# Moving the DRAM to DRAM copies of a rolling cache from the projection stage to the MLP stage, in eight rounds

## The reference

```
q, k, v  = project(rmsnorm(x))                       # one matrix, dilated heads a and differential heads b
h        = x + [dilated_attention(a), diff_attention(b)] @ w_out
y        = final_norm(h + relu(rmsnorm(h) @ w_up)**2 @ w_down)      # w_up 1024x4096, w_down 4096x1024
win_k_sample = concat(state_win_k, k_new)[:, 4:]     # (8, 2048, 512) float32; the same for v
```

## Time and profile before

| what | us |
|---|---|
| median of 3 runs (4608.19 to 4615.78) | 4612.5 |
| profiled execution, first to last instruction (span) | 4601.9 |
| projection / prompt attention / decode attention / MLP | about 712 / 1088 / 881 / 1921 |
| PE busy, of the span | 4152.4 (90%) |
| DVE / ACT / POOL busy | 2403.4 / 1536.3 / 805.8 |
| DMA traffic over the span | 686.79 MB, mean 149 GB/s |

### The profile page before, as it was taken

How to read it: one execution, slowest core, us unless ns; L and a number is a source line. 1 busy time by engine, 2 the same in 40 slices (tenths; PEclk the granted TensorE clock), 3 DMA queues, 4 the chain that set the end, 5 groups by cost and what they waited for, 6 DMA issues and landing times. The chain is left out here.

```text
span 4601.9 us, 72420 instructions
## 1 busy us (share of the span) xinstructions
PE 4152.4 (90%) x22272; PEld 3160.3 (69%) x22272; DVE 2403.4 (52%) x5184; ACT 1536.3 (33%) x2569; POOL 805.8 (18%) x694
## 2 busy tenths in 40 slices
PE   7996998999989897888888879999999998999998
PEld 6875884445444444445444458988988997998898
DVE  3333334756677684444444435565565555555654
ACT  2221224555545443223322332233223223223322
POOL 0001000000000000333333322222222222222121
PEclk9997999999999998999999989999999999999999
DMA  5756623110111103999999953324333333332231
GB/s 187 234 194 211 228 76 86 36 37 8 36 35 37 36 10 114 376 330 350 365 348 349 360 171 120 116 95 128 127 100 113 124 110 103 125 118 99 94 125 61
DMA packets 347208, 686.79 MB, mean 149 GB/s; under 512 B 27769, under 2 KB 185465, under 8 KB 343610
## 3 DMA queue, kind: packets, MB, share of 16 engines
q1 hardware_dynamic: 291295, 448.03, 29.3%
q0 software_dynamic: 47488, 218.01, 13.3%
q10 hardware_dynamic: 8155, 17.77, 1.4%
HBM read 632.85 MB, written 117.70 MB: 163 GB/s over the span
## 5 line engine op out<-in xcount | busy, mean ns | idle before, releaser
L1379 POOL TENSOR_TENSOR d_up_lo<-d_up_raw,d_up_hi 128x2048 fp32r<-128x2048 f32 x100 | 460.6, 4606 | 1420.3 <-ACT d_up_hi L1516 1420.3
L1384 PE MATMUL d_ups<-d_a_hi,d_up_hi 128*128 128x416 f32 x1600 | 568.2, 355 | 16.9 <-DVE d_a_lo L1671 16.2
L1386 PE MATMUL d_ups<-d_a_hi,d_up_lo 128*128 128x416 f32 x1600 | 566.1, 354 | 0.0
L836 POOL DMA_DIRECT2D c_v<-in_v_cache x512 | 275.2, 537 | 1638.9 <-issue 1627.8
L1385 PE MATMUL d_ups<-d_a_lo,d_up_hi 128*128 128x416 f32 x1600 | 560.6, 350 | 0.0
L530 PE MATMUL b_s<-b_k,b_q 128*128 128x512 f32 (+3 forms) x1280 | 498.5, 547 | 54.1 <-DVE b_part L662 30.6
L1384 PE MATMUL d_dps<-d_u_hi,d_down_hi 128*128 128x416 f32 x1280 | 461.7, 361 | 57.6 <-DVE d_y L1696 55.8
L1696 DVE TENSOR_TENSOR d_y<-d_y,d_dps 128x416 f32<-128x416 f32 x640 | 367.9, 584 | 225.6 <-PE d_dps L1386 223.6
L1386 PE MATMUL d_dps<-d_u_hi,d_down_lo 128*128 128x416 f32 x1280 | 458.2, 358 | 0.0
L1385 PE MATMUL d_dps<-d_u_lo,d_down_hi 128*128 128x416 f32 x1280 | 454.0, 355 | 0.0
L530 PEld LDWEIGHTS b_s<-b_k,b_q 128*128 128x128 f32 x1280 | 236.6, 197 | 291.0 <-issue 191.1
(11 more groups left out here) (164 smaller groups left out, 6306.4 us busy)
## 6 DMA issues: line engine op xcount, KB each, us to landing
c_k<-in_k_cache SPq DMA_DIRECT2D x512, 256.0 KB, 6.2
c_v<-in_v_cache POOLq DMA_DIRECT2D x512, 256.0 KB, 5.7
d_down_raw<-in_w_down SPq DMA_DIRECT2D x80, 1024.0 KB, 5.1
d_up_raw<-in_w_up SPq DMA_DIRECT2D x80, 1024.0 KB, 7.3
out_ka_win<-in_ka_state POOLq DMA_DIRECT2D x8, 4064.0 KB, 14.6
out_va_win<-in_va_state POOLq DMA_DIRECT2D x8, 4064.0 KB, 26.5
d_up_raw<-in_w_out SPq DMA_DIRECT2D x20, 1024.0 KB, 7.5
a_x<-in_x_prompt SPq DMA_DIRECT2D x32, 512.0 KB, 4.1
```

The lines of the kernel that those rows point to most:

```text
L836: eng.dma_start(dst[i][:, g, :], io[src[0]][bass.ds(page, 1)].rearrange("o p d -> (o p) d")).then_inc(landed[i], 16)
L1379: nc.gpsimd.tensor_tensor(up_lo[i][:], up_raw[i][:], up_hi[i][:].bitcast(F32), ALU.subtract).then_inc(up_lo_ready, 1)
L1384: nc.tensor.matmul(dst, w_hi, x_hi, start=first, stop=False)
L1386: return nc.tensor.matmul(dst, w_lo, x_hi, start=False, stop=last)
```

## The change

The copies, their four DMAs for each sample and their issuing engine stay as they are. They leave POOL's program in `project` and come into POOL's program in `mlp`: sample n's copy is issued right before the column groups 12n to 12n + 11 (`rounds` is 6 pairs of groups), so sample 0's at the very start of the stage. Four groups are left after the last round, then POOL waits for all copies. The body of the loop over column groups becomes the helper `cols_lo`, unchanged. The copies no longer wait for `xs_ready`, and POOL's wait for `w_ready[0]` in `project` goes with them.

```diff
@@ project, pool @@
-                body = (WIN - TD) // 16 * 16
-                pool.wait_ge(w_ready[0], NG)
-                def copy_window(n):
-                    pool.wait_ge(xs_ready, n * 3 + 5)
-                    for k in ("ka", "va"):
...
-                with pool.Fori(0, ND // 2) as n:
-                    copy_window(n)
                 for i in range(NG):
                     pool.wait_ge(w_hi_ready, NG + i + 1)
                     nc.gpsimd.tensor_tensor(w_lo[i][:], ...).then_inc(w_ready[1], 1)
-                with pool.Fori(ND // 2, ND) as n:
-                    copy_window(n)
-                pool.wait_ge(copied, 16 * 4 * ND)
@@ mlp, pool @@
-                with pool.Fori(0, NB * SG // 2) as q:
+                body = (WIN - TD) // 16 * 16
+                rounds = NB * SG // (2 * ND)
+                def copy_window(n):
+                    for k in ("ka", "va"):
+                        src = io[k + "_state"][bass.ds(n, 1)].rearrange("o t n -> (o t) n")
+                        dst = io[k + "_win"][bass.ds(n, 1)].rearrange("o t n -> (o t) n")
+                        pool.dma_start(dst[0:body].rearrange("(a b) n -> a b n", a=16),
+                                       src[TD:TD + body].rearrange("(a b) n -> a b n", a=16)).then_inc(copied, 16)
+                        pool.dma_start(dst[body:WIN - TD], src[TD + body:WIN]).then_inc(copied, 16)
+                def cols_lo(n, i):
+                    pool.wait_ge(up_hi_ready, n + (i + 1))
+                    pool.sem_inc(pool_gate, 1)
+                    nc.gpsimd.tensor_tensor(up_lo[i][:], up_raw[i][:], up_hi[i][:].bitcast(F32),
+                                            ALU.subtract).then_inc(up_lo_ready, 1)
+                for n in range(ND):
+                    copy_window(n)
+                    with pool.Fori(n * rounds, (n + 1) * rounds) as q:
+                        for i in range(2):
+                            cols_lo(q * 2, i)
+                with pool.Fori(ND * rounds, NB * SG // 2) as q:
                     for i in range(2):
...
+                        cols_lo(q * 2, i)
+                pool.wait_ge(copied, 16 * 4 * ND)
```

More of the change, by code:

```diff
@@ L125, in project @@
         VEC = 2 * NR + 1 + 2
-        copied = sem("a_copied")
         w_cols = io["w_in"].rearrange("(c p) (g n) -> g p c n", p=P, n=GW)
@@ L1283, in mlp @@
         sp_gate, pool_gate = sem("d_sp_gate"), sem("d_pool_gate")
+        copied = sem("d_copied")
         col_group = lambda b, s: s + b * SG
```

## The result

The changed kernel takes 4702.2 us (4 runs, 4699.6 to 4705.0), the kernel before, measured beside it, 4610.3 (4606.4 to 4615.8): ratio 1.0199, 95% interval [1.0185, 1.0214]. That is +92 us; the forecast was +63, 4676 us with a range of 4635 to 4735. The direction and the range hold. The difference is half as large again as forecast.

The account below looks back on a forecast made before the run. PE was taken as busy nearly throughout, so edits count by the PE waits they change. 27 + 20 + 30 + 8 + 0 = 85 us added, 21.8 given back: +63 on 4612.5, 4676 us, range 4635 to 4735.

Parts of the forecast that it names:

- The gain in the projection: Projection, samples 4 and 5: ACT's wait for an x tile behind two copies goes, giving back 21.8 us, bounds 15 to 25.
- One packet each in turn: DMA engines alternate one small load packet with each large copy packet, nearly freezing loads until 28 us after the copy's issue.
- Rival B: MLP stage: loads get some ten packets a turn, so copies cost 32 less 21.8 us, 4623 us; chance 0.07.
- The start, 27 us: MLP stage's start, sample 0: SP's first loads wait behind the copy, moving the start by 27 us, bounds 20 to 30.
- Samples 2 and 7, 15.1 us each: Behind the last `w_out` group: column group 5's load lands 15.1 us late, holding ACT's cast ahead of the last square and root.
- Samples 1, 3 and 6, 6.6 us each: Steady MLP loop: a late `down_raw` load makes PE wait 5.0 us, plus 1.6 for the clock; bounds 0 and 45 together.
- D = T0 + 29.4: Steady loop: landing time of the `down_raw` load, 29.4 us after T0, the copy's first issue; 9.3 us late.
- D + 8.0: Steady loop: end of the first `add`, 8.0 us after the load lands, through ACT's cast, DVE's subtraction and `split_u`.
- The clock term: Steady loop, samples 1, 3 and 6: the clock slows behind PE's wait, costing some 1.6 us more each.
- Sample 4, 8 us through the output store: Block 1's output stores: the store ends some 9.6 us later, PE waits 6.6 us plus 1.6 for the clock; bounds 0 and 15.
- A: Rival: PE loses 20 us or more at each of the eight copies, +153 us, 4765 us; chance 0.09.
- C: Rival: loads pass the copies, so all eight cost less than the 21.8 us given back; 4591 us with nothing lost; chance 0.05.

Follow-up runs that it names:

- e7: Kernel before the change, its copies in the projection cut into 4 KB packets: 4583.9 us, ratio 0.9955.
- e8: Kernel before the change, 65 KB packets kept, copies of samples 4 to 7 issued four steps later in the projection so none overlap: 4583.7 us, ratio 0.9959.
- e1: Changed kernel without the copies of the old window rows, so those output rows aren't written: 4581.6 us, ratio 0.9949 to the kernel before.
- e4: Changed kernel with the same bytes copied at the same places in 4 KB packets instead of 65 KB: 4628.6 us, ratio 1.0049 to the kernel before.
- e5: Changed kernel with the same bytes copied at the same places in 16 KB packets: 4664.0 us, ratio 1.0131 to the kernel before.
- e2: Changed kernel with sample 0's copy back in the projection, the other seven in the MLP stage: 4672.9 us, ratio 1.0141 to the kernel before.
- e10: Changed kernel with ACT's cast of column group 5 moved behind the root and the casts of `a_hi`: 4662.2 us, ratio 1.0128 to the kernel before.
- e3: Changed kernel with POOL's subtraction of a column group waiting until DVE has split the row group before it: 4683.8 us, ratio 1.0173 to the kernel before.
- e6: Changed kernel with 65 KB copies in 16 rounds, k and v apart, one before every sixth column group: 4606.8 us, ratio 1.0011 to the kernel before.
- e9: Changed kernel with 16 pieces of 65 KB packets, all issued in the steady loops of blocks 0 to 3: 4583.7 us, ratio 0.9950 to the kernel before.

## Why the prediction was right, and where its sizes were off

- *The gain in the projection*: 21.8 us by the rows, 22 in the profile after, 20 with e7 and e8. The 23.4 us between e1 and the kernel before hold more than the projection: 2.5 of them are in the MLP stage by the count above. Right, and e7 and e8 show both halves of its cause.
- *One packet each in turn, so loads are frozen until the copy ends*: right, shown by e4 and e5 at two other sizes. Rival B, where loads get some ten packets for one of the copy's, falls with it.
- *The start, 27 us*: 26.8 in the table, and e2 takes just this away. The size is right, but the path was not quite the one given. The prediction had all of SP's first loads in the queue with a dozen packets through by T0 + 28; in fact SP was held in its issue of the first constant, and the other two constants went out only from 2694.14 on, 27.65 us after the copy. With 4 KB packets (e4) that first issue took 5.89 us and the start still lost 23.3, so the held issue isn't needed for the loss; how much of it the hold makes with 65 KB packets is open.
- *Samples 2 and 7, 15.1 us each*: 17.7 and 18.3. The load landed at T0 + 31.8, not 30.9, and some 2 us come later, in groups 26 and 27. The mechanism, ACT's order, is shown by e10.
- *Sample 5, nothing*: right.
- *Samples 1, 3 and 6, 6.6 us each*: 13.1, 13.1 and 14.0. This is the step that failed in size. "D = T0 + 29.4" was 31.2. By T0 + 28 SP's queue had moved 160 packets, 10 an engine, just as forecast; but the copy's v part landed only at T0 + 28.2 and its 12-row tail at T0 + 30.3, and the last six packets an engine took some 3 us and not 1. And in "D + 8.0" the two halves of `split_u` were taken at their undisturbed 1.55 us each. ACT casts the next columns right behind the late rows, so that POOL subtracts beside `split_u` and DVE stands still for 4.2 us: D + 12.2 less 32.4 is 11.0, and PE waited 10.72. e3 shows that this part is POOL. The Trainium skill states the rule (SBUF — State Buffer, Who interferes with whom): a DVE instruction with two SBUF inputs contends with a GpSimd instruction that reads SBUF, and the second blocks fully until the first ends. The trace agrees, 4.76 against 0.59 us. The prediction had followed the late load along each engine's own program, but not asked which engines would now run side by side. The clock term was small as well: from 2933 to 2950 us the mean granted clock was 0.70, and 13.1 less 10.7 leaves 2.4 us where 1.6 was forecast. Over the whole stage the forecast had 6.4 us for the clock, and PE was busy for 12.9 us more.
- *Sample 4, 8 us through the output store*: 15.4, and the named mechanism didn't occur. The store had gone ahead of the copy's first packets. Its successors and the copy and SP's load then shared the engines as three queues, which put the copy's v part at 29.9 us and the `down_raw` load at T0 + 36.9. That the third queue is the reason for the later landing is read from the trace; no run took the stores away. DVE was held here too: its cast took 4.56 us where an undisturbed one takes 0.38, and e3 takes 5.2 us of this place away.
- *Rivals*: A (a full freeze at each copy, +153) is excluded by sample 5 and by e6, C (faster) by the start alone. C's other half is true, though: e9 shows that copies in this stage can cost nothing.

In sum, samples 1, 3 and 6 are 20 us over their forecast, sample 4 is 7 and samples 2 and 7 are 6; less the 2.5 us of the count's base this is the 31 us between 85 and 116. The projection gave back what was forecast. By the traces the sum is so 31 us short; by the medians, 92 against 63, it is 29. The range held because its bounds for samples 1, 3 and 6 went up to 45; the forecast's own sum did not foresee that POOL would hold up DVE.

## What to carry to other kernels

Here a large DRAM to DRAM copy took turns with a load, packet by packet, and its turns were as long as its packets: count the packets of the load, multiply by the time of one of the copy's, and set that against the margin of the load's consumer. Then cut the copy in pieces shorter than the margin, or into smaller packets, or put it where nothing that it meets is awaited; moving it whole to a stage with a lower DMA share says nothing. When something comes late, ask which engines run side by side from then on, and what else stands behind the waiting instruction in its program.

## What the hardware showed that was not expected

- In both kernels with 4 KB packets, only at the eighth sample, POOL's third DMA issue came late, behind an idle time of 19.13 us in e4 and 15.59 us in e7; with 65 KB or 16 KB packets no issue did. Why it is the eighth was not tried.
- SP's issue of a 4 KB constant took 27.04 us while the first copy ran, and one of an x load 16.05 us at sample 2: so an engine that issues a DMA is held too while a large copy runs. The same issue of the constant took 2.77 us with no copies (e1), 5.89 with 4 KB packets (e4), 16.82 with 16 KB (e5) and 13.70 beside a 65 KB copy of half the length (e6). Which queue limit does this was not tried.
